# Fourth chunk's first weight unit moved to second place, first transfer of x split in two

## What is computed

```
h = rms_norm(x, norm_gain)                        # x is 256 x 2048
proj = h @ w_in                                   # w_in is 2048 x 13392
(qa, ka, va, ga, qi, ki, wi, qb, kb, vb, gb, ma, mb) = split(proj)
...   # indexer top-k attention (branch A), differential attention (branch B)
merged = sigmoid(ma) * (oa*silu(ga) @ w_o_a) + sigmoid(mb) * (ob*silu(gb) @ w_o_b)
out = x + merged @ w_out
```

## Time and profile before

| | us |
|---|---|
| median of 3 runs (lowest, highest) | 770.45 (770.39, 770.49) |
| time of the profiled execution | 770.51 |
| span of its trace | 768.7 |
| PE busy | 764.8 (99% of the span) |
| DVE, ACT, POOL busy | 516.9, 431.1, 135.8 |

### The profile page before, as it was taken

How to read it: one execution, slowest core, us unless ns; L and a number is a source line. 1 busy time by engine, 2 the same in 40 slices (tenths; PEclk the granted TensorE clock), 3 DMA queues, 4 the chain that set the end, 5 groups by cost and what they waited for, 6 DMA issues and landing times.

```text
span 768.7 us, 10429 instructions
## 1 busy us (share of the span) xinstructions
PE 764.8 (99%) x3568; PEld 643.8 (84%) x3568; DVE 516.9 (67%) x724; ACT 431.1 (56%) x710; POOL 135.8 (18%) x225
## 2 busy tenths in 40 slices
PE   9999999999999999999999999999999999999998
PEld 8899988888888888888888888888888888888887
DVE  6768788888776755678656665767465567765553
ACT  6855756676663745555656565455576334444331
POOL 4412533322221000000212222312110011110000
PEclk9999999999999999999999999999999999999999
DMA  8988889998888675666866768767767888887553
GB/s 294 318 258 276 264 245 291 276 254 266 245 245 243 187 200 167 193 192 172 240 207 197 222 192 270 234 185 222 224 208 224 302 230 240 246 242 230 198 183 122
DMA packets 89612, 176.80 MB, mean 230 GB/s; under 512 B 7616, under 2 KB 15424, under 8 KB 89312
## 3 DMA queue, kind: packets, MB, share of 16 engines
q1 hardware_dynamic: 80752, 152.06, 65.8%
q0 software_dynamic: 8528, 23.87, 10.9%
q10 hardware_dynamic: 288, 0.30, 0.1%
HBM read 162.18 MB, written 14.02 MB: 229 GB/s over the span
## 4 chain that ended last, share of the span: by engine, by line
PE 99%; DMA 0%; DVE 0%; issue 0%
PE ps L760 29%; PE ps L762 29%; PE ps L761 29%; PE ps L774 1%; PE ps L778 1%; PE ps L794 1%; PE ps L795 1%; PE ps L784 1%; PE ps L860 0%; PE ps L963 0%; PE ps L962 0%; PE ps L961 0%; DMA xt<-in_x_columns 0%; PE ps L780 0%; PE ps L776 0%; PE ps L861 0%
## 5 line engine op out<-in xcount | busy, mean ns | idle before, releaser
L1332 DVE TENSOR_TENSOR lo<-raw,hi 128x1024 fp32r<-128x1024 f32 (+2 forms) x277 | 331.2, 1202 | 230.1 <-ACT hi L1041 229.3
L1041 ACT ACTIVATE hi<-raw 128x1024 fp32r<-128x1024 f32 (+2 forms) x277 | 286.3, 1038 | 291.5 <-PE ps L762 254.7
L760 PE MATMUL ps<-hi,hT_hi 128*128 128x512 f32 (+1 forms) x880 | 339.9, 386 | 0.0
L761 PE MATMUL ps<-lo,hT_hi 128*128 128x512 f32 (+1 forms) x880 | 339.0, 385 | 0.0
L762 PE MATMUL ps<-hi,hT_lo 128*128 128x512 f32 (+1 forms) x880 | 339.0, 385 | 0.0
L762 PEld LDWEIGHTS ps<-hi,hT_lo 128*128 128x128 f32 x880 | 165.2, 188 | 32.1
L760 PEld LDWEIGHTS ps<-hi,hT_hi 128*128 128x128 f32 x880 | 165.2, 188 | 31.5
L761 PEld LDWEIGHTS ps<-lo,hT_hi 128*128 128x128 f32 x880 | 165.2, 188 | 31.3
L760 PE MATMUL ps<-hi,ogT_hi 128*128 128x512 f32 x128 | 49.8, 389 | 0.0
L761 PE MATMUL ps<-lo,ogT_hi 128*128 128x512 f32 x128 | 49.8, 389 | 0.0
L762 PE MATMUL ps<-hi,ogT_lo 128*128 128x512 f32 x128 | 49.8, 389 | 0.0
(11 more groups left out here) (199 smaller groups left out, 665.1 us busy)
## 6 DMA issues: line engine op xcount, KB each, us to landing
raw<-in_w_in SPq DMA_DIRECT2D x190, 512.0 KB, 4.5
raw<-in_w_out SPq DMA_DIRECT2D x32, 512.0 KB, 4.2
raw<-in_w_o_a SPq DMA_DIRECT2D x16, 512.0 KB, 5.9
raw<-in_w_o_b SPq DMA_DIRECT2D x16, 512.0 KB, 4.2
raw<-in_w_in SPq DMA_DIRECT2D x16, 384.0 KB, 4.9
turned<-swapped POOLq DMA_DIRECT2D x12, 512.0 KB, 3.3
v<-turned POOLq DMA_DIRECT2D x32, 128.0 KB, 5.8
raw<-in_w_in SPq DMA_DIRECT2D x7, 336.0 KB, 4.6
```

What stands on the lines that cost most here:

```text
L760: mm(o, a_hi, w_hi[:, j], start=first and j == 0, stop=False)
L761: mm(o, a_hi, w_lo[:, j], start=False, stop=False)
L1041: activation(hi[:, slot, :, 0:width], raw[:, slot, :, 0:width], ACT.Copy).then_inc(hi_ready, 1)
L1332: tt(lo[:, slot, :, 0:width], raw[:, slot, :, 0:width], hi[:, slot, :, 0:width].bitcast(F32), ALU.subtract).then_inc(lo_ready, 1)
```

## The change

Unit (3,0) stands second in `FIRST_UNITS`, and `EARLY` is 4, so that four units come in halves. The loops over chunk 3 begin at i = 1. The places of the first index chunk's take-out and of its rotation's first two steps move by one, since one more unit stands ahead of them. `gain` and `freq` change places in `x_columns`, and the first transfer of x comes in two, both from ACT's queue: first the second row tile (128 columns) with the gain, then the frequencies with the first row tile. DVE makes `hT_hi` of the two row tiles apart, and PE waits for the second of these ahead of the first row tile's matmuls. One small row of constants is loaded a place earlier, and the positions come behind the first transfer of the ring's second turn.

```diff
-EARLY = 3
+X_FIRST = HD // 2
+X_HALF = X_FIRST + P
+EARLY = 4
...
-FIRST_UNITS = ((2, 0), (0, 0), (1, 0))
+FIRST_UNITS = ((2, 0), (3, 0), (0, 0), (1, 0))
...
-INDEX_OUT = (2 * CK + 4, 3 * CK + 2)
-INDEX_ROPE = ((2 * CK + 5, 2 * CK + 6, 3 * CK, 3 * CK + 1), (3 * CK + 3, 3 * CK + 5, 3 * CK + 6, 3 * CK + 7))
+INDEX_OUT = (2 * CK + 5, 3 * CK + 2)
+INDEX_ROPE = ((2 * CK + 6, 2 * CK + 7, 3 * CK, 3 * CK + 1), (3 * CK + 3, 3 * CK + 5, 3 * CK + 6, 3 * CK + 7))
...
-            for u in range(EARLY, 3 * CK):
+            for u in range(EARLY, len(FIRST_UNITS)):
...
-                if u == EARLY + 1:
+                if u == EARLY:
                     sp.dma_start(pos_i[:, :], positions).then_inc(phases_landed, 16)
...
-                for i in range(CK):
+                for i in range(1 if c == 3 else 0, CK):
...
                 if c >= PACKED:
+                    if k == 0:
+                        pe.wait_ge(x_hi_first, 2)
                     mm(o_0, hT_hi[:, k, 0:P], w_hi, start=first, stop=False)
...
-            at = slice(0, X_FRONT + X_CUTS[1] * S)
-            act.dma_start(xt[:, at], x_columns[:, at]).then_inc(x_landed[0], 16)
+            for at, landed in ((slice(X_HALF, X_FRONT + S), x_half_landed), (slice(0, X_HALF), x_landed[0])):
+                act.dma_start(xt[:, at], x_columns[:, at]).then_inc(landed, 16)
...
             early_hi(0, 0)
+            act.wait_ge(x_half_landed, 16)
             act.wait_ge(x_landed[0], 16)
             x_hi_again(0).then_inc(x_again_first, 1)
...
-            dve.wait_ge(x_landed[0], 16)
-            ts(hT_hi[:, 0, :], x_tile(0), gainT[:, 0:1], None, ALU.mult).then_inc(x_hi_first, 1)
-            dve.wait_ge(x_hi_first, 1)
+            for rows, landed in ((slice(P, S), x_half_landed), (slice(0, P), x_landed[0])):
+                dve.wait_ge(landed, 16)
+                ts(hT_hi[:, 0, rows], x_tile(0)[:, rows], gainT[:, 0:1], None, ALU.mult).then_inc(x_hi_first, 1)
+            dve.wait_ge(x_hi_first, 2)
             x_lo_tile(0).then_inc(x_lo_first, 1)
```

More of the change, by code:

```diff
@@ L49 @@
 X_FRONT = KT + HD // 2
-EARLY = 3
+X_FIRST = HD // 2
+X_HALF = X_FIRST + P
+EARLY = 4
 SINES_AT = 12
 X_OWN_AFTER = ((3, 2), (3, 4), (3, 6), (4, 0))
-ROWS_AFTER = ((2, 5), (2, 6), (2, 7), (3, 0), (3, 1), (3, 3), (3, 5), (3, 7), (4, 1))
+ROWS_AFTER = ((2, 4), (2, 5), (2, 6), (2, 7), (3, 1), (3, 3), (3, 5), (3, 7), (4, 1))
 LO_STEP, LO_W = P + P // 2, P + P // 2 + P
@@ L127, with unit_width @@
 FIRST_UNITS += tuple((2, i) for i in range(len(THIRD_BEHIND), CK))
-assert len(FIRST_UNITS) == 3 * CK
+assert len(FIRST_UNITS) == 3 * CK + 1
+def unit_width(u):
+    return FIRST_W[FIRST_UNITS[u][0]] if u < len(FIRST_UNITS) else chunk_width(u // CK)
 def chunk_end(c):
@@ L241, in build_layer @@
         xt = sb("xt", [P, X_FRONT + KT * S], at=m_at)
-        gainT, freq = xt[:, 0:KT], xt[:, KT:X_FRONT]
+        gainT, freq = xt[:, X_FIRST + S:X_FRONT + S], xt[:, 0:X_FIRST]
         K_LO, Q_LO, K_FIRST = slice(0, S), slice(S, S + P), slice(S + P, CW)
@@ L264, in x_tile @@
         def x_tile(k):
-            return xt[:, X_FRONT + k * S:X_FRONT + (k + 1) * S]
+            first = X_FIRST if k == 0 else X_FRONT + k * S
+            return xt[:, first:first + S]
         va_hi, va_lo = qk_hi[:, 0:4, :].rearrange("p b s -> p (b s)"), v_r[:, 0, 0:A_W]
@@ L421, in build_layer @@
         T0, S0 = 4, 6
+        x_half_landed = sem("x_half_landed")
         x_landed = [sem(f"x_landed_{i}") for i in range(len(X_CUTS) - 1)]
@@ L1043, in make_hi_ahead @@
             def make_hi_ahead(c, i):
-                width = chunk_width(c + (i + RING) // CK) if isinstance(c, int) else CW
+                width = unit_width(c * CK + (i + RING)) if isinstance(c, int) else CW
                 make_hi(c * CK + (i + RING), i % RING, c * 2 + (i // RING + 1), width)
@@ L1773 @@
     freqs = (_np.float32(10000.0) ** -exponents).astype(_np.float32)[None]
-    x_columns = _np.concatenate([_np.asarray(inputs["norm_gain"])[0].reshape(KT, P).T,
-                                 _np.broadcast_to(freqs, (P, HD // 2)),
-                                 _np.asarray(inputs["x"])[0].T.reshape(KT, P, S).transpose(1, 0, 2).reshape(P, KT * S)],
-                                axis=1)
+    x_tiles = _np.asarray(inputs["x"])[0].T.reshape(KT, P, S).transpose(1, 0, 2).reshape(P, KT * S)
+    x_columns = _np.concatenate([_np.broadcast_to(freqs, (P, HD // 2)), x_tiles[:, 0:S],
+                                 _np.asarray(inputs["norm_gain"])[0].reshape(KT, P).T, x_tiles[:, S:]], axis=1)
     laid_out = {"x_columns": x_columns, "positions": _np.asarray(inputs["positions"])[0].reshape(RT, P).T}
```

## The result

The changed kernel takes **771.91 us** (median of 14 runs, 770.63 to 773.09) against 770.47 before (14 runs beside them, 770.17 to 771.61). The ratio is 1.0017, with a 95% interval of 1.0010 to 1.0024. It is slower by about 1.4 us, where the prediction had 770.3 and a range up to 771.1. Its runs are spread over 2.5 us, those of before mostly over 0.8. The profiled execution took 772.34 us, its span is 770.5, so 1.8 us over the span of before.

A forecast was written before the change was run, and what follows sets the result against it. PE, 99% busy, was taken as the bound, leaving only its stalls to gain. The terms -0.31 + 0.13 + 0 = -0.18 us gave 770.3 us, range 769.8 to 771.1.

The forecast's parts named there:

- Step 2: Kernel start, x in two pieces: second piece lands at 4.04 (3.85 to 4.24), +0.13 us (ends -0.06 and +0.33).
- The even trade: Rival, 12%: x's second piece lands at 4.24 or later, its +0.33 eats the 0.31 gain; 770.4 to 770.65.
- The early pieces: Rival, 8%: at the start, x's second piece lands at 3.5 if time goes by size; -0.64 us in all, 769.8.
- Step 3: Ring's second turn: the stall at (1,1) near 13.4 us goes, as PE needs it only at 15.66; -0.31 us.
- Step 4: Ring's second turn: (0,1) waits for a slot, is issued at 8.00, lands at 12.0, 0.27 us in time; 0 us.
- The step's own sign of being wrong: Ring's second turn: the forecast for (0,1) is wrong if ACT's rounding of it begins after 12.3.
- Step 1: Units' order: moving (3,0) up front costs nothing in itself, the same 2.11 us of PE as today.
- step 5: Hidden edits (phases and sines, first rotation, constants row, positions): covered by existing slack, nothing priced.
- What would show it: Signs of a right forecast: matmul starts in the first half-units, (0,1) issued near 8.0, no gap at (0,1) or (1,1).

The follow-up runs named there:

- SP silent: Changed kernel, but SP issues its second weight transfer only once x's second piece has landed; 772.86 us in its one execution.
- x whole: Changed kernel with x's first transfer in one piece again, unit (3,0) still second; 771.02 us, ratio 1.0004.
- one program: Kernel before with x's first transfer in two pieces and nothing else changed; 772.62 us, ratio 1.0016.
- swapped pieces: Changed kernel with x's two pieces issued in the other order, 96 KB first and 72 KB with the gain second; 771.10 us in its one execution.

## Why the prediction was wrong, point by point

**Step 2, the split: the price was taken from the wrong row, and the term left out the clock. This is the step that failed.** It priced the second piece at 2.9 us, after transfers issued first, at an empty queue. It was issued at 1.18, behind two others, with SP's next transfers under way beside it, and took 3.6, landing at 4.76. Even its upper end, 4.24, was too low: in the four profiles with this piece second and SP not held back it landed between 4.4 and 4.9. The trace of before had the right neighbour, which was not used, SP's second transfer (issues between 1.1 and 1.3 us, KB and us to landing):

```profile
raw<-in_w_in SPq DMA_DIRECT2D x1, 256.0 KB, 3.3
```

Issued at 1.18, it took 3.3 us, which alone gives a landing at 4.5. `hT_lo` came 0.84 us later, not 0.13. The same step said of the sooner first matmul that it "gains nothing". It cost: it cut PE's work in two. The second matmul came 1.12 us behind the first, where the half pace takes 0.28, and the clock stayed low until 8.9 us. The half pace is 0.45 + 0.87 = 1.3 us in the profile and 0.9 in the medians.

**The rivals.** The even trade named the right mechanism, "it now shares the DMA engines with SP's second and third transfers". Its price was too low and its chance, 12%, too small. The early pieces were wrong here, and their landing at 3.5 was given without a working. The Trainium skill's fixed cost, which that rival took as its mechanism ("DMA: Bandwidth & Descriptors", Anatomy of one DMA), stands there for transfers that GpSimd issues; it makes 2.2 us of 96 KB by an estimate from that page, where the piece took 2.6 with SP silent. The trace does not agree with it even for a first transfer: x's first piece, 72 KB, took 2.8 us, where the same estimate gives 2.2. No rival had the clock, though the change visibly put a wait right behind the warm-up.

**Step 3, the gap of 0.31 us at (1,1):** gone in the changed kernel, but behind a PE that was 2 us late. With x whole it came back larger, 0.8 us with that at (0,1), and two more profiles of the kernel before (one with an eighth warm-up matmul) had none. A gap seen in one execution was counted as the kernel's own.

**Step 4, (0,1) near 8.0:** its issue came at 9.02, and at 8.84 with x whole. The subtraction's place was priced rightly. In the changed kernel the issue came 1.70 us later than the 7.32 of before: 0.84 is x's lateness again, 0.31 DVE's wait for the third transfer, and the 0.55 left is the subtraction. With x whole the wait was 0.92 (timeline of DVE in the changed kernel, then with x whole):

```profile
6.80 1.34 DVE L1478 TENSOR_TENSOR lo<-raw,hi 128x512 fp32r<-128x512 f32 x2 [0.31 <-ACT hi L1033]
```
```profile
6.59 1.36 DVE L1472 TENSOR_TENSOR lo<-raw,hi 128x512 fp32r<-128x512 f32 x2 [0.92 <-ACT hi L1029]
```

So what was missed besides x was the third transfer, at 4.2 to 4.4 us instead of 3.4. The step's own sign of being wrong came true: ACT's rounding of (0,1) began at 12.81, and at 12.50 with x whole, after the 12.3 given (timeline of ACT in the changed kernel):

```profile
12.81 1.06 ACT L1054 ACTIVATE hi<-raw 128x1024 fp32r<-128x1024 f32 x1 [1.41 <-DMA raw<-in_w_in]
```

(0,1) took 3.8 us, less than the 4.0 forecast; it was its issue that came late. PE, itself late by then, did not wait for it. The DMA stood half idle for 2.5 us ahead of this issue and behind it. Step 3 allowed (1,1) 5.5 us, and with x whole it took 5.6 (issued at 9.77, rounded from 15.45).

**Step 1 and step 5 held.** (3,0)'s odd half took 1.07 us of PE up front. No start was late between 18 and 73 us, so rotation, sines and small rows were covered in this execution.

**What would show it:** the first matmul near 4.30 (4.01), the x lo product near 4.94 (5.65), the 384-wide half-unit at 5.77 (6.93). The chance for "within 0.2%" was 95%, and the median moved by 0.19%, just inside, which is luck: the clock, the larger part of it, was in no term and in no rival.

## What to carry to other kernels

Price a transfer by a neighbour at the same place in the queue, not by the first one, and remember that a second queue shares the same engines. In the first microseconds an early start of PE that was followed by a wait was worse here than a later start without one (771.91 against 770.96 with nine warm-up matmuls); keep the warm-up running until the data is certain to be there. Here a ring whose slots are all filled by small early pieces left the DMA half idle until the first was free.

## What the runs showed of the hardware that was not expected

The view of stretches prints a granted clock of 1.00 for the changed kernel at 6.93 to 8.85 us, where its matmuls go at half pace (0.32 us for 384 columns):

```profile
6.93:8.85 1.92, 1.92 (x7) 1.92 (x7) 1.92 (x4) 1.92 (x6) 0.00 (x0) 1.00 0.97 371
```

So the start of a kernel has to be judged by the matmuls' starts and not by that column. The page's busy share of 99% did not show it either. And eight of twelve executions of one program took 772.2 to 773.3 us and four 770.7 to 771.0, which fits a clock that in some executions rises in spite of the pause. Only one of the twelve was profiled, so this is argued and not shown. The swapped pieces, with the higher level right behind a pause of 0.79 us, are one profiled execution of that kind in a kernel near to it. And once the higher level was there, a longer pause did not cost it: with SP silent PE idled for 1.17 us ahead of its matmul at 6.87, and the next ones of 384 columns started 0.17 to 0.18 us apart.
